# Each unit of weights in two transfers of 512 KB in place of one of 1 MB, in the same queue

## The reference, cut to what matters

```python
h = rms_norm(x, pre_norm_g[l])
u = jnp.einsum('bsd,de->bse', h, w_in[l])
...
y = jnp.concatenate([o_a, o_b, o_c, o_d], axis=-1) * jax.nn.silu(u_gate)
y = jnp.einsum('bse,ed->bsd', y, w_out[l])
x = x + rms_norm(y, post_norm_g[l])
```

## Time and profile before

| | us |
|---|---|
| median of 3 runs | 1141.62 |
| lowest, highest | 1139.51, 1143.92 |
| profiled execution, its own time | 1142.56 |
| its span, from the first to the last instruction | 1140.8 |
| TensorE busy | 1054.2 |
| VectorE busy | 576.9 |
| ScalarE busy | 167.6 |
| GpSimd busy | 25.0 |

### The profile page before, as it was taken

One profiled execution on the slowest core, in us unless ns is written; L12 is line 12 of the kernel. 1 busy time (PEld: TensorE's weight loads), 2 busy tenths in 40 slices (PEclk: granted clock), 3 DMA queues, 4 the chain that ended last, 5 costly groups with the idle time before them and its releaser, 6 DMA issues. The chain is left out here.

```text
span 1140.8 us, 12128 instructions
## 1 busy us (share of the span) xinstructions
PE 1054.2 (92%) x4160; PEld 727.2 (64%) x4160; DVE 576.9 (51%) x1383; ACT 167.6 (15%) x402; POOL 25.0 (2%) x42
## 2 busy tenths in 40 slices
PE   3999994999999999996899999989999799999993
PEld 2858752758756757645566666668886476666661
DVE  2595625495734342528665666764332443332347
ACT  1124212015311231100000000001332000000000
POOL 2000000000000000000200000000010000000000
PEclk9999997999998999898899999989999899999997
DMA  6654454544456355244766666624333334444430
GB/s 250 227 217 176 158 219 163 221 184 184 184 180 261 114 219 184 74 187 155 303 223 252 260 232 246 258 74 148 133 124 111 111 147 174 158 163 168 149 146 37
DMA packets 29168, 204.63 MB, mean 179 GB/s; under 512 B 3422, under 2 KB 3459, under 8 KB 5452
## 3 DMA queue, kind: packets, MB, share of 16 engines
q1 hardware_dynamic: 26796, 191.60, 45.1%
q0 software_dynamic: 2336, 12.58, 2.9%
HBM read 203.11 MB, written 1.05 MB: 179 GB/s over the span
## 5 line engine op out<-in xcount | busy, mean ns | idle before, releaser
L1296 PE MATMUL bank<-hT,raw 128*128 128x256 f32 x2176 | 485.6, 382 | 5.5 <-DMA raw<-units_dram 4.9
L1296 PEld LDWEIGHTS bank<-hT,raw 128*128 128x128 f32 x2176 | 414.0, 191 | 81.2 <-issue 21.8
L1306 PE MATMUL bank<-raw,yT 128*128 128x512 f32 x224 | 99.4, 602 | 2.3 <-DVE yT L1198 2.0
L1010 DVE SCALAR_TENSOR_TENSOR ada<-raw,cact,ada 128x256 f32<-128x256 f32 (+1 forms) x168 | 81.5, 485 | 6.0
L1537 PE MATMUL bank<-raw,arena 128*128 128x512 f32 x180 | 82.1, 592 | 0.0
L1306 PEld LDWEIGHTS bank<-raw,yT 128*128 128x128 f32 x224 | 42.8, 192 | 55.3 <-issue 52.9
L1306 PE MATMUL bank<-raw,hT 128*128 128x512 f32 (+1 forms) x192 | 74.9, 549 | 2.6 <-DVE hT L808 2.6
L597 ACT ACTIVATE arena<-bank 128x512 f32<-128x512 f32 x32 | 19.1, 598 | 394.2 <-PE bank L1296 394.2
L1065 DVE TENSOR_TENSOR arena<-arena 128x512 f32<-128x512 f32 x32 | 22.1, 691 | 86.4 <-ACT arena L597 86.1
L729 DVE SCALAR_TENSOR_TENSOR ada<-raw,cact,ada 128x1024 f32 x42 | 53.9, 1283 | 22.6 <-DMA raw<-units_dram 21.7
L1306 PEld LDWEIGHTS bank<-raw,hT 128*128 128x128 f32 x192 | 36.2, 190 | 39.6 <-issue 33.2
(11 more groups left out here) (285 smaller groups left out, 966.2 us busy)
## 6 DMA issues: line engine op xcount, KB each, us to landing
raw<-units_dram SPq DMA_DIRECT2D x180, 1024.0 KB, 4.8
arena<-ln_rows_dram POOLq DMA_DIRECT2D x4, 1024.0 KB, 6.4
arena<-ada_rows_dram POOLq DMA_DIRECT2D x1, 2048.0 KB, 7.4
arena<-att_line_dram POOLq DMA_DIRECT2D x1, 2048.0 KB, 15.5
arena<-small_dram POOLq DMA_DIRECT2D x2, 896.0 KB, 6.3
xt<-x_dram SPq DMA_DIRECT2D x1, 1024.0 KB, 4.9
arena<-post_g_dram POOLq DMA_DIRECT2D x2, 512.0 KB, 8.6
out_dram<-xt SPq DMA_DIRECT2D x1, 1024.0 KB, 4.0
```

The source lines that it names most:

```text
L1010: ins = dve.scalar_tensor_tensor(dst, w, cact[:, k:k + 1], dst, ALU.mult, ALU.add)
L1296: mm = pe.matmul(b[:, c * S:(c + 1) * S], raw[:, s, k * 256 + c * P:k * 256 + (c + 1) * P], act_t[:, k, :], start=(k == 0), stop=(k == KC ...
L1306: mm = pe.matmul(banks[t][:, 0:width], act_t[:, 4 * half + k, t * P:(t + 1) * P], raw[:, s, k * 512:k * 512 + width], start=(half == 0 and ...
```

## The change

Each unit is fetched by two transfers of [128, 1024], first the left half of each partition's row and then the right one, both by SP and both adding 16 to the slot's `landed`. The consumers wait for 32 times the count, so for both halves. The loop issues both behind the same wait for `used`. Nothing else differs.

```diff
         def wait_landed(eng, turns, n):
-            eng.wait_ge(landed[n % SLOTS], 16 * (turns + n // SLOTS + 1))
+            eng.wait_ge(landed[n % SLOTS], 32 * (turns + n // SLOTS + 1))
...
+            HALVES = [slice(h * (UNIT // 2), (h + 1) * (UNIT // 2)) for h in range(2)]
             for s in range(SLOTS):
-                sp.dma_start(raw[:, s, :], units[s, :, :]).then_inc(landed[s], 16)
+                for c in HALVES:
+                    sp.dma_start(raw[:, s, c], units[s, :, c]).then_inc(landed[s], 16)

             with sp.Fori(1, N_UNITS // SLOTS) as i:
                 for s in range(SLOTS):
                     sp.wait_ge(used[s], i)
-                    sp.dma_start(raw[:, s, :], units[i * SLOTS + s, :, :]).then_inc(landed[s], 16)
+                    for c in HALVES:
+                        sp.dma_start(raw[:, s, c], units[i * SLOTS + s, :, c]).then_inc(landed[s], 16)
```

## The result

The changed kernel takes 1154.59 us (median of 4 runs, 1153.32 to 1159.81) against 1140.57 of the kernel before (4 runs, 1137.75 to 1143.92). The ratio is 1.013, with an interval from 1.0088 to 1.0173. The forecast was 1144.0 us, with a range from 1140.5 to 1149.5.

What follows compares the result with a forecast made beforehand. TensorE, busy 1054.2 of 1140.8 us, was taken as the bound. Terms 0.9 (six waits), 0.2 (units behind another) and 1.2 (collision) sum to 2.3 us, giving a median of 1144.0 us, range 1140.5 to 1149.5.

Steps and rivals of the forecast that it cites:

- the cost of a unit behind another: Units issued right behind another: their data waits for the first one's anyway, so 0.2 us in all was added.
- the six waits: Four in the first block's layers, one starting the feed-forward groups, one at 734.38: each grows by 0.15, 0.9 us together.
- the pair is the nearest row: Two whole units issued 0.5 us apart, the second landing 2.5 us after the first: taken as evidence for d = 0.15.
- d: How much later a whole unit lands when fetched as two halves: forecast 0.15 us, bounds -0.1 and 2.1 us paid again.
- two small ones cost what one large one does: Weights' queue: two 4 KB packets (0.168 us each) cost one of 8 KB (0.339), adding 0 to 0.1 us to d.
- the collision: Unit issued at 546.4 shares the engines with GpSimd's bias line; smaller packets make it 1.2 us later, bounds 0 and 3.
- The clock: Behind the wait for the unit issued at 546.4, an 8 us stretch mostly at 1.2 GHz was expected again, as long.
- the slack of w1: First feed-forward, 13 groups: w1 lands about 0.55 us before TensorE's first load on it, so it pays nothing.
- The tail: Second feed-forward: two kinds of units share three slots and none of the counted waits for weights lies there.
- SyncE's extra issues: 180 more issues of 407 ns, 73 us over the run on a mostly waiting sequencer, costed at nothing by itself.
- The packets' count: Weights' queue: some 25,900 packets more, 180 x 128 of data and 180 x 16 semaphore writes, with the same bytes.
- the part that is not data is paid again, in part: Rival: d near 1, the 13 feed-forward groups wait 5.9 us, 15 us in all, 1157 us; chance 0.11.

Runs made afterwards that it cites:

- Block halves: Against the kernel before: each unit by two transfers, each half one 512 KB block in memory, both waited for; 1151.15 us, ratio 1.0091.
- One transfer with small rows: Kernel before, still one transfer per unit, but with packets of 4 KB; 1144.61 us, ratio 1.0035.
- its repetition: The changed kernel run again beside the kernel before, with more runs; 1154.46 us, ratio 1.0105.
- the loop written out: The changed kernel with SyncE's counted loop written out, fixed addresses for its 354 transfers; 1152.61 us, ratio 1.0099 to the kernel before.
- its written-out loop: The kernel before, whole units, with SyncE's counted loop written out; 1141.01 us, ratio 0.9995.
- the delay of 0.36 us: Kernel before with six semaphore increments on SP between the wait for a slot and each unit's issue; 1142.79 us, ratio 1.0021.
- halves in the tail alone: Kernel before with two transfers only for units from 132 on (attention and second feed-forward); 1140.66 us, ratio 0.9994.
- the delay of 1.2 us: Kernel before with 20 semaphore increments on SP between the wait for a slot and each unit's issue; 1162.03 us, ratio 1.0155.
- a probe of a full queue on a quiet core: Kernel before plus, after its output, five groups of six back-to-back transfers of different shapes; 1209.43 us including them; four block halves landed after 7.16 us.
- Cut by partitions: Against the kernel before: each unit by two transfers of 64 partitions each, rows kept at 8 KB; 1231.31 us, ratio 1.0778.

## Why the prediction was wrong

- **The step that failed** is the cost of a unit behind another: "For units behind another I add 0.2 us in all". It rests on "its data has to wait for the first one's anyway", which holds only while the queue runs dry nowhere. Measured, each second unit lands 1.2 us later. In the profile that makes 3.8 us of standstill, the norm's 1.1 through VectorE with it, where the sum had 0.65 (0.2 and three of the six waits at 0.15), and it opened new waits (86.55 and 263.99, whose units had 0.9 us of slack before). Block halves show it by themselves: units alone earlier than before, second units 1.1 us later, and 10 us lost. The reason for the late third transfer is open.
- **The reading behind it** is "since the pair is the nearest row". The pair in the trace was two transfers of a megabyte, and was read as proof that everything but data overlaps. Halves behave differently: a unit alone measured d = 0.38 in place of 0.15, inside the bounds given.
- **The packets**: "two small ones cost what one large one does" came from one microsecond. One transfer with small rows cost 0.35%, 4 us, though its landings moved by up to 0.1 and 0.2 only. Its profile has 1.7 us more standstill than before, 1.2 of it at the collision; the rest of the 4 isn't explained.
- **The places**: six waits were named. Five of them grew (36.01, 44.25, 213.65, 221.74, 746.66), the one at the start of the groups isn't there (nor does TensorE wait for weights there in the trace of before), and five came that were not named (86.55, 263.99, 449.21, 608.87, and the norm through VectorE).
- **The clock** was looked at behind the collision alone, and put at nothing. 4.0 us of the profiled loss are matmuls at the lower clock (half of it read from durations alone), and not there: that stretch was shorter. They stand in the first unit of each layer of the first block, 9.73 us before. In all four traces in which every unit comes as two halves and is waited for whole (this one, its repetition, block halves, the loop written out) both such units are slow, 11.3 to 11.8 us; in the kernel before, its written-out loop, the delay of 0.36 us and the small rows neither is. But with halves in the tail alone, where these units come whole, one of them is slow as well (11.94), so chance has a part in it, and how the halves bring it about no run shows.
- **Held**: the slack of w1. The groups' 38 units are issued within 162.0 us (161.3 before), and the delay of 1.2 us, not that of 0.36, moved them. The tail paid nothing. A term that the sum hadn't: two units alone, at 449.21 and 608.87, that took 8.1 and 6.5 us cost 2.3 us. The collision's wait grew by 0.96 (1.2 forecast), but the unit behind it ran in 8.55 us in place of 10.07, so it cost nothing in sum. No cost of SyncE's extra issues was seen: bringing the halves 0.15 us closer by writing out the loop changed nothing. The packets' count was exact.
- The rival "the part that is not data is paid again, in part" gave 1157 us, close to the result. It was right that a piece returns, but for other places: it put the loss into the 13 groups, which didn't wait. Its price for d = 1, 15 us, agrees with the delay of 1.2 us (17.7 us measured). The Trainium skill's "DMA: Bandwidth & Descriptors", section "Anatomy of one DMA", was taken as a reason for an estimated 2.0 us more per unit; the trace shows 0.38 and 1.2, between that and nothing. Its direction was right, and 0.11 for a partial price was too little weight for it.

## What to carry to other kernels

Cutting a transfer is not free even where one unit alone hides it: price the transfer that is queued behind another separately, for it moved three times as far as the lone one (1.2 against 0.38 us). Measure the lateness inside the kernel, since a probe of a full queue on a quiet core showed none for block halves. A cut can pay only if someone starts on the first piece: block halves, which lost 0.9% while both were waited for, won 0.5% so. Whether halves in rows with gaps would win too wasn't tried.

## What the runs showed that was not expected

- A half of 512 KB in rows with gaps lands after 3.9 us, the same half as one block after 3.24 (medians, units alone).
- Cut by partitions, packets of the same 8 KB take 612 ns (median) in place of 309, and the queue is busy 69.1% of the span for the same bytes.
- Semaphore increments on SyncE follow one another every 60 ns, though each is busy for 17.
- A halved row costs DMA time with gaps (49.3%) and, less, within one transfer (47.1%), but hardly any as blocks (45.5%, before 45.1%).
